# A feed-forward down projection rewritten as seven block products with 256 tokens moving, its weight sums made by GpSimd during the up projection

## The reference

```python
def swiglu(h, w_gate_up, w_down):
    g, u = jnp.split(h @ w_gate_up, 2, axis=-1)
    return (jax.nn.silu(g) * u) @ w_down
...
        h = rms_norm(x, g_ffn_pre[l])
        x = x + rms_norm(swiglu(h, w_gate_up[l], w_down[l]), g_ffn_post[l])
```

## Time and profile before

| | us |
|---|---|
| median of 3 runs | 1463.74 (1463.42 to 1464.24) |
| the profiled execution, device time | 1463.54 |
| its span in the trace | 1461.7 |
| what lies around the span | 1.84 |
| TensorE busy | 1449.6 (99% of the span) |
| stage `ffn_up`, TensorE's stretch | 449.40 to 688.80 |
| stage `ffn_down`, TensorE's stretch | 688.80 to 808.50 |
| from there to the first matmul of `dil_in` | 808.50 to 818.33 |

### The profile page before, as it was taken

How to read it: one execution, slowest core, us unless ns; L and a number is a source line. 1 busy time by engine, 2 the same in 40 slices (tenths; PEclk the granted TensorE clock), 3 DMA queues, 4 the chain that set the end, 5 groups by cost and what they waited for, 6 DMA issues and landing times.

```text
span 1461.7 us, 21937 instructions
## 1 busy us (share of the span) xinstructions
PE 1449.6 (99%) x8234; PEld 1208.5 (83%) x8234; DVE 897.9 (61%) x1389; ACT 616.6 (42%) x960; POOL 242.0 (17%) x215
## 2 busy tenths in 40 slices
PE   9999999999999999999999899999999999999999
PEld 6888779898899888888888688888888888888787
DVE  6524673566638655455323787747666866767878
ACT  6222775453345222223223542334665433334654
POOL 0200102020020000000000565545522110110000
PEclk9999999999999999999999999999999999999999
DMA  5622103422023665754422122232203333334643
GB/s 177 202 87 93 53 2 122 138 87 87 1 87 116 204 186 185 223 175 155 166 86 90 55 87 90 96 103 87 60 2 87 87 91 110 86 98 132 223 152 122
DMA packets 159251, 164.06 MB, mean 112 GB/s; under 512 B 7357, under 2 KB 134589, under 8 KB 157765
## 3 DMA queue, kind: packets, MB, share of 16 engines
q1 hardware_dynamic: 157268, 159.84, 34.5%
q0 software_dynamic: 848, 3.17, 0.6%
q10 hardware_dynamic: 1056, 0.00, 0.0%
HBM read 149.33 MB, written 13.65 MB: 111 GB/s over the span
## 4 chain that ended last, share of the span: by engine, by line
PE 96%; DVE 2%; POOL 1%; DMA 0%; ACT 0%; issue 0%; SPq 0%; DVEq 0%; ACTq 0%; POOLq 0%
PE ps L2259 27%; PE ps L2261 27%; PE ps L2260 27%; PE ps L2696 3%; PE ps L2785 1%; PE ps L2803 1%; PE ps L2886 1%; PE ps L2895 1%; PE ps L2706 1%; PE ps L547 1%; POOL x_t L863 1%; DVE w_lo L2169 1%; DMA raw<-in_w_in 0%; PE ps L2727 0%; PE ps L2954 0%; PE ps L2955 0%
## 5 line engine op out<-in xcount | busy, mean ns | idle before, releaser
L2259 PE MATMUL ps<-a_hi,w_hi 128*128 128x512 f32 (+2 forms) x1576 | 588.6, 373 | 4.9 <-POOL w_lo L811 2.3
L2261 PE MATMUL ps<-a_hi,w_lo 128*128 128x512 f32 (+2 forms) x1576 | 583.3, 370 | 0.0
L2260 PE MATMUL ps<-a_lo,w_hi 128*128 128x512 f32 (+2 forms) x1576 | 583.0, 370 | 0.0
L2259 PEld LDWEIGHTS ps<-a_hi,w_hi 128*128 128x128 f32 (+1 forms) x1576 | 296.2, 188 | 61.3 <-DVE a_lo L1626 4.2
L2261 PEld LDWEIGHTS ps<-a_hi,w_lo 128*128 128x128 f32 (+1 forms) x1576 | 296.2, 188 | 51.6
L2260 PEld LDWEIGHTS ps<-a_lo,w_hi 128*128 128x128 f32 (+1 forms) x1576 | 296.3, 188 | 50.9 <-issue 0.7
L949 ACT ACTIVATE w_hi<-raw 128x2048 fp32r<-128x2048 f32 x105 | 200.8, 1913 | 254.6 <-PE ps L2261 240.2
L1511 DVE TENSOR_TENSOR w_lo<-raw,w_hi 128x2048 fp32r<-128x2048 f32 x85 | 194.6, 2289 | 154.2 <-ACT w_hi L949 153.7
L811 POOL TENSOR_TENSOR w_lo<-raw,w_hi 128x2048 fp32r<-128x2048 f32 x22 | 101.4, 4608 | 435.7 <-ACT w_hi L949 408.0
L2017 DVE TENSOR_TENSOR arena<-ps,rstd 128x512 f32<-128x512 f32 x88 | 59.8, 687 | 137.6 <-PE ps L2261 132.6
L2259 PE MATMUL ps<-w_hi,a_hi 128*128 128x512 f32 x346 | 135.6, 392 | 1.3 <-DVE w_lo L2169 0.9
(11 more groups left out here) (279 smaller groups left out, 1542.8 us busy)
## 6 DMA issues: line engine op xcount, KB each, us to landing
raw<-in_w_gate_up SPq DMA_DIRECT2D x44, 512.0 KB, 5.6
raw<-in_ffn_w_up SPq DMA_DIRECT2D x44, 512.0 KB, 4.7
raw<-in_attn_w_in SPq DMA_DIRECT2D x36, 512.0 KB, 4.5
raw<-in_w_in SPq DMA_DIRECT2D x24, 512.0 KB, 4.7
arena<-in_ffn_w_down SPq DMA_DIRECT2D x24, 512.0 KB, 4.1
sums_dram<-arena SPq DMA_DIRECT2D x11, 1024.0 KB, 3.9
raw<-in_w_down SPq DMA_DIRECT2D x22, 512.0 KB, 4.4
raw<-in_w_mem_kv SPq DMA_DIRECT2D x16, 512.0 KB, 4.4
```

Of the source, the lines that this page charges most:

```text
L2259: pe.matmul(dst, s_hi, m_hi, start=start, stop=False, skip_group_check=across)
L2260: pe.matmul(dst, s_hi, m_lo, start=False, stop=False, skip_group_check=across)
L2261: return pe.matmul(dst, s_lo, m_hi, start=False, stop=stop, skip_group_check=across)
```

## The change

`ffn_down` is rewritten. The 1024 output features, the 2816 hidden features and the 512 tokens are each cut in two, and the product of the 2x2 blocks is made with seven block products in place of eight (sums and differences of weight blocks against sums and differences of hidden blocks, then sums of the products). Weights stay stationary in tiles of 128x128; 256 tokens move. There are 29 steps: 11 pair steps of 48 matmuls (four products, four feature tiles, three passes; two PSUM banks for each product) and 18 single steps in three runs of six (two operands, four feature tiles, three passes, 24 matmuls; the last of each run has one operand, 12 matmuls). That is 11 x 48 + 15 x 24 + 3 x 12 = 924 matmuls 128x256, where 528 matmuls 128x512 were.

The weight sums are made in `ffn_up` by GpSimd: for each of 11 pairs of depth tiles it issues two loads of 512 KB, four additions 128x512, and a store of 1 MB to `sums_1_dram`; and for each pair of hidden tiles two additions 128x256 (`basis`, now on the same engine between the pairs). SP's new `load_down` waits for all eleven stores before it loads step 0. Steps use a ring of four raw buffers and the two slots of `w_hi` and `w_lo`.

VectorE makes the sums of hidden blocks and their `lo` parts, joins finished products during the later steps and adds squares up as they come. In the tail the last pieces are squared, `by_token` for the part known earlier stands ahead of step 28, one last copy of 128x1024 to `y_ffn` stands on ScalarE ahead of the split of the second `dil_in` chunk, and the gain moves from ScalarE's copy into VectorE's scaling.

```diff
-    ("ffn_up", 22, 2, 2, "dve"), ("ffn_down", 11, 1, 0, ""),
+    ("ffn_up", 22, 2, 2, "dve"), ("ffn_down", 29, 1, 0, ""),
...
+            def load_down():
+                for t in DOWNS:
+                    if t.c < 2:
+                        sp.wait_ge(weights_split, t.g + CREDIT - 1)
+                    elif t.c < 4:
+                        sp.wait_ge(hidden_written, CREDIT + FT)
+                    else:
+                        sp.wait_ge(weights_split, t.g + CREDIT - 3)
+                    if t.c == 0:
+                        sp.wait_ge(rel_moved, SUMS_1_MOVED + 48 * PAIRS_K)
+                    if t.first:
+                        sp.dma_start(t.q[:, 0, :], w_down_1[t.pair, 0][:, 0:512]).then_inc(t.landed, 16)
+                        sp.dma_start(t.q[:, 1:3, :], sums_1_dram[t.pair, :, 0:2, :]).then_inc(t.landed, 16)
+                        sp.dma_start(t.q[:, 3, :], sums_1_dram[t.pair, :, 3, :]).then_inc(t.landed, 16)
...
+            def sums_of_quarters(pair):
+                b11, b12, b21, b22 = (quarter_set_1[:, n, :] for n in range(4))
+                pool.wait_ge(rel_moved, SUMS_1_MOVED + 48 * pair)
+                for k in range(2):
+                    pool.dma_start(quarter_set_1[:, 2 * k:2 * k + 2, :],
+                                   w_down_1[pair, k].rearrange("p (q n) -> p q n", n=512)).then_inc(rel_moved, 16)
+                pool.wait_ge(rel_moved, SUMS_1_MOVED + 48 * pair + 32)
+                pool.tensor_tensor(b22, b22, b12, ALU.subtract).then_inc(quarter_sums_1, 1)
+                pool.tensor_tensor(b12, b12, b11, ALU.subtract).then_inc(quarter_sums_1, 1)
...
+                pool.tensor_tensor(b11, b22, b11, ALU.add).then_inc(quarter_sums_1, 1)
...
+                pool.tensor_tensor(b21, b21, b11, ALU.subtract).then_inc(quarter_sums_1, 1)
...
+                pool.dma_start(sums_1_dram[pair], quarter_set_1).then_inc(rel_moved, 16)
...
+            for t in DOWNS[:PAIRS_K]:
+                sums_of_quarters(t.pair)
+                if t.pair:
+                    basis(DOWNS[t.pair - 1])
+            basis(DOWNS[PAIRS_K - 1])
             split_lo(Chunk(G["dil_in"], 0, 6, 0))
...
+            for t in DOWNS[2:]:
+                operands_hi(t)
+                if t.c + 1 < DOWN_STEPS:
+                    sides_hi(DOWNS[t.c + 1])
...
+            split_hi(Chunk(G["ffn_down"], 0, 2, DOWN_STEPS - 1))
...
+                act.activation(token_squares(1)[:, 2 * h:2 * h + 2, :], bank_quarter(P1_1)[:, 2 * h:2 * h + 2, :],
+                               ACT.Square).then_inc(post.sq, 1)
+            root_of(post, ps[:, 4, 0:4])
+            act.wait_ge(product_joined, 2)
+            act.activation(y_quarter(0, 0), bank_quarter(P1_1), ACT.Copy).then_inc(post.sq, 1)
             split_hi(Chunk(G["dil_in"], 0, 6, 0))
...
+            def operands_lo(t):
+                dve.wait_ge(weights_hi, t.g + 1)
+                dve.tensor_tensor(t.weight(w_lo), t.q[:, 0:t.many, :], t.weight(w_hi).bitcast(F), ALU.subtract)\
+                   .then_inc(weights_split, 1)
...
+                if t.c - RUNS[0] in (1, 2, 3):
+                    join_down(t.c - RUNS[0])
...
+                        for a, w, bank in t.products():
...
+                            for f in range(4):
+                                cols = slice(f * 128, f * 128 + 128)
+                                last = three(feature_quarter(bank, f), (whi[:, w, cols], wlo[:, w, cols]),
+                                             (hi[:, a:a + 256], lo[:, a:a + 256]), t.c == 0 and f % 2 == 0,
+                                             t.pair == PAIRS_K - 1, across=True)
...
+                    if ends:
+                        pe.wait_ge(norms["ffn_post"].added, CREDIT + 7)
+                        by_token(square_sum, True, False)
```

More of the change, by code:

```diff
@@ L42, with step_loads, ring_loads, raw_shift @@
 ]
+PAIRS_K = FT // 2
+DOWN_STEPS = 29
+DOWN_RING = 4
+def step_loads(c):
+    return 48 if c < PAIRS_K else 32
+def ring_loads(buffer, until=DOWN_STEPS):
+    return sum(step_loads(c) for c in range(buffer, until, DOWN_RING))
+def raw_shift(slot, chunk0):
+    return ring_loads((slot - chunk0) % 2) - 32 * len(range((slot - chunk0) % 2, DOWN_STEPS, 2))
 class Gemm:
@@ L60, in plan @@
     return gemms, chunk
+DOWN_CHUNK0 = plan()[0]["ffn_down"].chunk0
+RAW_SHIFT = [raw_shift(slot, DOWN_CHUNK0) for slot in range(2)]
 class Chunk:
@@ L343, in __init__ @@
-                self.w = (G["conv_up"].chunk0 + FT + c) % 2
+                self.landed = CONV_LANDED[self.buffer]
+                self.landed_at = CONV_LANDED_0[self.buffer] + sum(step_loads(d) for d in range(self.buffer, c + 1, 5))
+                self.q = CONV_BUFFERS[self.buffer]
+                self.g = TOTAL + c
                 self.many = 4 if self.first else 3
-                self.operands = self.many * 512
-                self.sides_done = 2 * (c + 1) if self.first else 2 * PAIRS_K + (c - PAIRS_K + 1)
@@ L2631, in stay_clocked @@
                 for _ in range(n):
-                    pe.matmul(ps[:, 6, :], w_hi[:, ch.slot, 0:128], w_hi[:, ch.slot, 0:S], start=True, stop=True,
+                    pe.matmul(ps[:, 3, :], w_hi[:, ch.slot, 0:128], w_hi[:, ch.slot, 0:S], start=True, stop=True,
                               skip_group_check=True)
-            def summed_but_last(norm):
-                pe.wait_ge(norm.added, CREDIT + KT - 1)
-                by_token(square_sum, True, False)
             def summed(norm, then):
-                pe.wait_ge(norm.sq, KT)
-                by_token(squares[:, 3, :], False, True).then_inc(norm.sum, 1)
+                for f in range(4):
+                    pe.wait_ge(norm.sq, 4 + f // 2)
+                    for b in range(2):
+                        last = pe.matmul(ps[:, 4, b:b + 1], token_squares(1)[:, f, b * 128:b * 128 + 128], ones[:, 0:1],
+                                         start=False, stop=f == 3, skip_group_check=True)
+                last.then_inc(norm.sum, 1)
                 stay_clocked(then, 5)
@@ L2872, in _ @@
             feature_major("ffn_up", "", peel=2, tail=1)
[L2873 to L2876 removed]
+            seven_products_by_feature()
             summed(norms["ffn_post"], "dil_in")
```

443 lines of the change are left out of this document (288 added, 155 removed).

## The result

The changed kernel takes a median of 1470.61 us (1467.58 to 1474.84, seven runs), the kernel before 1464.10 (1463.42 to 1464.42, seven runs). The ratio is 1.0047, with an interval of 1.0034 to 1.0060: slower by 0.47%. That lies inside the predicted range, 0.4 under its upper end and above the likeliest case. The profiled execution of the changed kernel is the slowest of the seven, 1474.84 us with a span of 1473.0, 11.3 more than the span before.

What follows compares the result with a forecast made beforehand. The prediction took TensorE, busy 99% of the span, as the bound. 1463.54 less 3.3 gained in `ffn_down` with its tail plus 4.4 lost in `ffn_up` gave 1464.6, or 1464.8 us against the median; range 1459.0 to 1471.

Steps and rivals of the forecast that it cites:

- the likeliest case: Whole kernel: the forecast itself, 1462 to 1466.7 us with a tail above; chance 0.38.
- additions that win every race: Rival, `ffn_up`'s opening: GpSimd's additions go ahead of VectorE's chain, 8 us likely, 10.4 at most; 1468.4; chance 0.12.
- single steps that lose more: Rival, `ffn_down`: 18 single steps each 0.25 us over their margin, 4.5 more, 1469; chance 0.07.
- the prediction's own signs: Profile after: `ffn_up` longer by 2 to 5 us before 475, later chunks unstretched, last store landed before SP waits.
- I cost this part at nothing: `ffn_up` in steady state: GpSimd keeps up, mid 18 us a pair against 21.76, so no loss.
- The opening: `ffn_up`'s start: GpSimd's additions hold up VectorE, 2.0 us at the first pair, 2.4 at the second, 4.4 lost.
- ffn_down itself: `ffn_down` before its tail: matmuls 110.9 us, new standstill 3.9, first `by_token` 0.95.
- the closing steps: `ffn_down`: the step behind a run's last waits 1.2 us; two such places give 2.4.
- step 1: `ffn_down`'s start: step 1 waits 0.9 us, its `w_hi` split standing behind a table load.
- the weight load's pace: Rival, `ffn_down`: narrow matmuls run at the 188 ns weight load, 54 us more, 1518; chance 0.02.
- The tail: Last down matmul to first `dil_in` matmul: 10.5 us for 9.83, root 0.4 earlier, copy adding 1.06.
- GpSimd falls behind: Rival, `ffn_up`: pairs take over 21.76 + 0.7 us, making `ffn_down`'s step 0 late; 1475 at 23.5 a pair; chance 0.07.

Runs made afterwards that it cites:

- SP's split order: Against the changed kernel, SP in `ffn_up` stores sums behind the even chunk's weights and loads quarters behind the odd chunk's; median 1468.48 us, ratio 1.0033.

## Why the prediction came out as it did

That the time falls inside the range is luck. The range's upper end stood for additions that win every race and for single steps that lose more, and neither came; the largest loss that came has no term in the sum. Two of the prediction's own signs speak against its working: a later part of `ffn_up` stretched, and the last store landed 9.2 us after SP began to wait for it.

The predicted sum was 1.1 us on the span (4.4 lost, 3.3 gained). The profiled execution has 11.3: 2.2 less at the opening, 6.4 more at the standstill, 2.5 less gained in `ffn_down` and its tail, 3.4 more at the second block's end (1.1 - 2.2 + 6.4 + 2.5 + 3.4 = 11.2).

- **The step that failed** is "I cost this part at nothing", on GpSimd's sums in `ffn_up` in its steady state. The working asked whether GpSimd keeps up with its own pairs, which it does, and raised the DMA share by 0.28, which is about what came behind the standstill (0.58 to 0.88). It did not ask what waits for a *landing* on the queue that carries the weights. The part cost 6.4. Rows of the kernel before show it (above): a split released by the weights' load, ready 1.4 ahead of TensorE's need, behind a store that SP waits for. Shown by four runs: no weight sums, no loss; their transfers without their additions, the same standstill; the two other orders on SP, 0.44 and nothing near 506. Of the margin, 1.0 was already taken by the `basis` additions beside VectorE's, which the working left out as well. That the standstill then costs another 2.4 at the lower clock was not foreseen either.
- **The opening.** Mechanism right (without additions, or with late ones, the loss is gone), size 2.2 for 4.4. A collision stretched `a_lo` to 1.33 once and to 0.72 three times, where 0.5 each and two delays of 1.30 were assumed; at the second pair one VectorE operation was hit, by 0.64.
- **ffn_down itself.** 116.3 for 115.75, and 115.6 with GpSimd's sums left out (127.98 less a tail of 12.4). The pitch of 0.120, the closing steps (1.24 for 1.2) and step 1 (0.98 for 0.9) came as worked out; the joins cost nothing in place of 0.6; step 2's load, 0.66, was missed. The rivals of the weight load's pace and of the single steps fell with this.
- **The tail.** Mis-sized, 12.5 for 10.5. The chain at its end was right, the copy's 1.06 measured 0.9 (10.7 to 9.8). Its start was wrong: the root stood not 0.4 earlier but 1.75 later (817.81, 4.14 behind the last matmul, for 2.39 before), because the squares ahead of it stand behind a split that waits for its load. With that load earlier, the tail took 10.7.
- **GpSimd falls behind** did not happen in the change, yet by little. Its pairs take 21.1 on the mean (first additions at 456.40 and, ten pairs later, 667.69; single ones from 15.5 to 24.3) in place of the mid of 18, against the 21.76 of two chunks. SP was ready to load step 0 from about 669.5, not from 677.9 as the working has it. Some 2 us of cover were left: the last store landed at 678.7, step 0's weights at 684.75, and ScalarE's split of step 0 at 686.76 was still released by TensorE, not by its load. With additions 22.7 later it happened as that rival says, with 8.3 us of standstill at step 0.

No version here that makes the sums beats the kernel before. The best ones, with one queue or load moved, are at 1467.9 to 1468.5; each further repair moved the lateness to another place. The two edits that helped, SP's split order and the earlier `dil_in` load, were not run together without the late additions. If they added up, `dil_in` would start at an estimated 692.35 + (822.16 - 695.93) = 818.6, for 818.33 before: about level. Whether the additions could be put by hand into VectorE's quiet stretches, with SP's order changed as well, was not tried. Why the load at the second block's end lands late in some executions stays open.

## What to carry to other kernels

Before work is put on an idle engine, look past that engine's own busy time: list what its transfers share, and in each in-order queue the waits for a landing, and find the item behind each with the smallest margin. A stage without a gap can sit 1.4 us from one, and the chain of waits doesn't show it; the releaser of the splits does. When an engine runs beside VectorE, its place in VectorE's cycle can matter more than its length: here a GpSimd freed of a wait made `ffn_up` 4.6 us longer (701.97 for 697.38).
